# Softmax normalisation moved from the probabilities to the attention outputs, in a two-layer hybrid diffusion block on one core

## What is computed

```python
s = jnp.concatenate([s_win, s_ctx, sink_col], axis=-1)      # sink_col in the windowed heads only
p = jax.nn.softmax(s, axis=-1).astype(q.dtype)
o = einsum(p[..., :span], vw) + einsum(p[..., span:span + nctx], vc)
```

## Time and profile before

| | us |
|---|---|
| three runs | 1332.77, 1341.63, 1337.88 |
| median | 1337.88 |
| profiled execution, its own time | 1334.14 |
| its span, first to last instruction | 1332.3 |
| attention of layer 0, first scores to first gate product | 153.7 to 242.9 |
| attention of layer 1, the same | 874.7 to 931.0 |

### The profile page before, as it was taken

One profiled execution on the slowest core, in us unless ns is written; L12 is line 12 of the kernel. 1 busy time (PEld: TensorE's weight loads), 2 busy tenths in 40 slices (PEclk: granted clock), 3 DMA queues, 4 the chain that ended last, 5 costly groups with the idle time before them and its releaser, 6 DMA issues.

```text
span 1332.3 us, 22176 instructions
## 1 busy us (share of the span) xinstructions
PE 1213.0 (91%) x8966; PEld 927.0 (70%) x8966; DVE 645.4 (48%) x1503; ACT 440.1 (33%) x1049; POOL 167.0 (13%) x208
## 2 busy tenths in 40 slices
PE   4899987999999999999999889999998878889986
PEld 2787854788888967666666459875998865555652
DVE  1544786464355463422221285587767645324334
ACT  3533366533334351010000265356666610000001
POOL 1810000110010210000000321000111100000001
PEclk9899999999999999999999999999999889999998
DMA  9995145423323269999999995338564989999995
GB/s 352 316 353 177 64 138 188 150 95 95 95 95 127 90 265 416 399 415 413 416 384 373 402 237 149 120 133 278 177 189 145 357 333 413 417 416 413 380 374 192
DMA packets 131831, 351.15 MB, mean 264 GB/s; under 512 B 23053, under 2 KB 84725, under 8 KB 108560
## 3 DMA queue, kind: packets, MB, share of 16 engines
q1 hardware_dynamic: 118144, 317.69, 64.4%
q0 software_dynamic: 12304, 30.37, 6.7%
q10 hardware_dynamic: 1280, 1.66, 0.4%
HBM read 330.53 MB, written 28.86 MB: 270 GB/s over the span
## 4 chain that ended last, share of the span: by engine, by line
PE 81%; DVE 10%; issue 4%; DMA 4%; ACT 2%; POOL 0%; SPq 0%; DVEq 0%; ACTq 0%; POOLq 0%
PE banks L1028 34%; PE banks L1286 16%; PE banks L1300 8%; PE banks L1278 6%; PE banks L1209 4%; PE banks L962 2%; PE banks L1134 2%; PE banks L1149 2%; PE banks L1119 1%; DMA expert_rows<-arena,rows_u 1%; DMA ring<-in_w_in 1%; DMA ring<-in_w_mod 1%; DVE w_lo_r L2042 1%; DVE arena L2461 1%; DVE att L2128 1%
## 5 line engine op out<-in xcount | busy, mean ns | idle before, releaser
L2042 DVE TENSOR_TENSOR w_lo_r<-ring,w_hi_r 128x256 fp32r<-128x256 f32 x480 | 223.0, 475 | 229.5 <-ACT w_hi_r L1641 228.3
L1641 ACT ACTIVATE w_hi_r<-ring 128x256 fp32r<-128x256 f32 x480 | 197.5, 416 | 302.5 <-PE banks L1028 255.3
L1286 PE MATMUL banks<-ring,arena 128*64 128x256 f32 x2016 | 232.5, 383 | 21.5 <-DVE arena L2429 8.6
L1028 PE MATMUL banks<-h_hi_r,w_hi_r 128*128 128x512 f32 (+1 forms) x640 | 221.9, 347 | 5.7 <-DVE h_lo_r L1988 5.6
L1028 PE MATMUL banks<-h_lo_r,w_hi_r 128*128 128x512 f32 (+1 forms) x640 | 220.2, 344 | 0.0
L1028 PE MATMUL banks<-h_hi_r,w_lo_r 128*128 128x512 f32 (+1 forms) x640 | 220.0, 344 | 0.0
L1286 PEld LDWEIGHTS banks<-ring,arena 128*64 128x64 f32 x2016 | 161.9, 138 | 81.7 <-issue 31.2
L1028 PEld LDWEIGHTS banks<-h_hi_r,w_hi_r 128*128 128x128 f32 x640 | 122.3, 191 | 22.2 <-ACT arena L1611 5.0
L1300 PE MATMUL banks<-ring,att 128*64 128x512 f32 x424 | 119.7, 609 | 15.2 <-issue 7.8
L1028 PEld LDWEIGHTS banks<-h_lo_r,w_hi_r 128*128 128x128 f32 x640 | 122.5, 191 | 13.9
L1028 PEld LDWEIGHTS banks<-h_hi_r,w_lo_r 128*128 128x128 f32 x640 | 122.4, 191 | 13.9
(11 more groups left out here) (274 smaller groups left out, 1704.3 us busy)
## 6 DMA issues: line engine op xcount, KB each, us to landing
ring<-in_w_e_gate SPq DMA_DIRECT2D x64, 1024.0 KB, 8.9
ring<-in_w_e_up SPq DMA_DIRECT2D x62, 1024.0 KB, 9.3
ring<-in_w_e_down SPq DMA_DIRECT2D x53, 1024.0 KB, 9.3
ring<-in_w_mod SPq DMA_DIRECT2D x48, 1024.0 KB, 6.5
ring<-in_w_in SPq DMA_DIRECT2D x38, 1024.0 KB, 5.6
expert_rows<-att POOLq DMA_DIRECT2D x23, 512.0 KB, 20.3
ring<-in_w_o SPq DMA_DIRECT2D x8, 1024.0 KB, 5.1
ring<-in_w_branch SPq DMA_DIRECT2D x8, 640.0 KB, 4.6
```

The costliest lines, as they stand in the source:

```text
L1028: ins = mm(out_ap, a, b, start=k == 0 and p_ == 0, stop=k == KD - 1 and p_ == 2)
L1286: ins = mm(banks[e * CAP:(e + 1) * CAP, bank, 0:DE], x[:, k, e * CAP:(e + 1) * CAP], w[:, k * DE:(k + 1) * DE], start=k == 0, stop=k == KD ...
L1641: fn(w_hi[:, u % AHEAD, :, :], chunk(key)[:, q * KU:(q + 1) * KU, :], ACT.Copy).then_inc(w_hi_ready, 1)
L2042: v.tensor_tensor(w_lo[:, u % AHEAD, :, :], chunk(key)[:, q * KU:(q + 1) * KU, :], w_hi[:, u % AHEAD, :, :].bitcast(F32), ALU.subtract).th ...
```

## The change

The probabilities stay unscaled. VectorE still takes the reciprocals of the row sums, and then one copy spreads the two reciprocals of a step (two blocks of 128 queries) over 64 columns each, into `recip`, a view of arena tile 4 with room for two pairs of steps. At the end of `attend`, PE makes two products of `recip` with the identity: they turn it, so that bank 6, columns 256 to 511, holds for each output row of the two heads the reciprocals along the queries. ScalarE copies the raw outputs to `arena` as before (now counted by `o_raw`), and VectorE multiplies them by these columns once for two steps, behind the maximum of the even iterations (`o_ready`). `turn_p` waits for the exponentials instead of the scaling. The stream of VectorE is one iteration longer. In iteration 1 VectorE waits for `y_a_ready`. `small_in` and `gate_a_in` become one counter each over both layers. Matmul shapes, score and value products, and everything outside attention are as before.

```diff
+        recip = arena[:, T_AC, :].rearrange("p (u b e m) -> p u b e m", u=2, b=2, e=2)
@@ small parameters and gate rows
-        small_in = [sem(f"small_in{l}") for l in range(DEPTH)]
+        small_in = sem("small_in")
-        gate_a_in = [sem(f"gate_a_in{l}") for l in range(DEPTH)]
+        gate_a_in = sem("gate_a_in")
-                pool.wait_ge(small_in[l], SMALL)
+                pool.wait_ge(small_in, SMALL * (l + 1))
-                dve.wait_ge(gate_a_in[l], 16 * (2 - l))
+                dve.wait_ge(gate_a_in, 16 * (2 + l))
@@ PE, turn_p
-                pe.wait_ge(p_ready, g + 1)
+                pe.wait_ge(exp_done, g + 1)
@@ PE, attend
+                pe.wait_ge(recip_ready, g + 2)
+                for b in range(2):
+                    ins = mm(banks[:, O_BANK, (2 + b) * P:(3 + b) * P],
+                             recip[:, g // 2 % 2, b, :, :].rearrange("p e m -> p (e m)"), ident, start=True, stop=True)
                 ins.then_inc(pv_done, 1)
@@ ACT, attention
-                        fn(arena[:, tn, q0:q0 + 2 * P], banks[:, O_BANK, 0:2 * P], ACT.Copy).then_inc(o_ready, 1)
+                        fn(arena[:, tn, q0:q0 + 2 * P], banks[:, O_BANK, 0:2 * P], ACT.Copy).then_inc(o_raw, 1)
@@ DVE, attention
                     if 0 <= s - 1 < n:
-                        b = (s - 1) % 3
-                        k = width(l, s - 1) - (STEPS[l][s - 1][0] == "win")
+                        if s == 1:
+                            dve.wait_ge(y_a_ready, 2 * (l + 1))
                         dve.wait_ge(exp_done, g)
-                        link(v.reciprocal(rsum[:, b, :], esum[:, b, :]))
-                        for q in range(2):
-                            ins = v.tensor_scalar(S[b][:, q, 0:k], S[b][:, q, 0:k], rsum[:, b, q:q + 1], None, ALU.mult)
-                        ins.then_inc(p_ready, 1)
+                        r = rsum[:, (s - 1) % 3, :]
+                        link(v.reciprocal(r, esum[:, (s - 1) % 3, :]))
+                        v.tensor_copy(recip[:, (g - 1) // 2 % 2, :, (s - 1) % 2, :], r.unsqueeze(2).to_broadcast([P, 2, HD]))\
+                            .then_inc(recip_ready, 1)
...
                             .then_inc(max_ready, 1)
+                    if s % 2 == 0 and 0 <= s - 4 < n:
+                        family, h, on_ctx = STEPS[l][s - 4]
+                        tn = T_NQ + h // 2 if family == "na" else T_WQ + h % 3
+                        q0 = SEQ if on_ctx else 0
+                        o = arena[:, tn, q0:q0 + 2 * P]
+                        dve.wait_ge(o_raw, (g - 4) // 2 + 1)
+                        v.tensor_tensor(o, o, banks[:, O_BANK, 2 * P:4 * P], ALU.mult).then_inc(o_ready, 1)
@@ DVE, main
-                attention(l, 2, len(STEPS[l]) + 2)
+                attention(l, 2, len(STEPS[l]) + 3)
```

More of the change, by code:

```diff
@@ L473, in program @@
         exp_done = sem("exp_done")
-        p_ready = sem("p_ready")
+        recip_ready = sem("recip_ready")
         p_turned = sem("p_turned")
@@ L478, in program @@
         pv_done = sem("pv_done")
+        o_raw = sem("o_raw")
         o_ready = sem("o_ready")
@@ L625, in small_loads @@
             ):
-                eng.dma_start(dst, src).then_inc(small_in[l], 16)
+                eng.dma_start(dst, src).then_inc(small_in, 16)
         def load_rev(eng, l, heads=range(H_NA)):
@@ L934, in _ @@
                     pool.wait_ge(y_gated, QT0[1])
-                rows_in(l, 2, gate_bc, gate_a_in[l])
+                rows_in(l, 2, gate_bc, gate_a_in)
                 merge(l)
```

## The result

| | before | changed |
|---|---|---|
| median of 18 runs each (us) | 1335.61 | 1340.28 |
| lowest to highest | 1332.7 to 1342.2 | 1337.3 to 1344.66 |
| ratio, 95% interval | | 1.0033, 1.0019 to 1.0047 |
| profiled execution: own time, span | 1334.14, 1332.3 | 1344.66, 1342.8 |
| attention of layer 0 (first scores to first gate product) | 89.17 | 94.92 |

A forecast was written before the change was run, and what follows sets the result against it. The prediction took a loop of waits through `attend` to bound layer 0, with PE full in layer 1; 14 x 0.47 = 6.6 less 1.0 at the starts gave +5.6 us, forecast 1343.5, range 1334 to 1352.

The forecast's parts named there:

- The loop: Layer 0 latent pair: `attend`, turn, context scores, their copy, maximum, exponentials, copy of PT follow without idle, 8.05 us.
- Scaling, 0 in steady state, -0.52 at each start: Scaling gone from VectorE: hidden by 0.03 us in steady state; the second maximum starts 0.52 us earlier in each layer.
- Products, 0.47 a pair: Two identity products on PE at the end of `attend`, on the loop: between 0.39 and 0.66 us, taken as 0.47.
- Spreading copy, 0.20: VectorE's copy spreading the reciprocals, 0.20 us in a row, replacing 0.83 of scaling: 0 on the path.
- Output product, hidden with 0.2 of cover: VectorE's output product delays its copy of PT, but ScalarE's copy ends 0.2 us later: cost 0.
- Rival 3: Output product holds VectorE's queue, delaying PT's copy and `attend`; products may be dearer: +13.8 us, 1351.7, chance 0.11.
- The sum over the intervals: 10 `attend` intervals in layer 0 and 4 in layer 1, each +0.47: 6.6 us.
- The ends: Last stretch of each attention stage: the win at `turn_p` is taken back by the last products, about 0.
- Rivals 1, 2 and 4: 1: normalisation on path, 1334.7, chance 0.10; 2: VectorE bound, 1325.4, 0.08; 4: products under other PE work, 1336.9, 0.05.
- Rival 2: VectorE bounds the latent steps, so time goes with its work: -12.5 us, 1325.4, chance 0.08.

The follow-up runs named there:

- the second timing: The changed kernel, unaltered, timed again beside the two new orders against the kernel before: 1341.29 us, ratio 1.0037.
- the new order: Kernel before, PE's odd iterations with turn and context scores first, `attend` last, third PT buffer, ScalarE's output copy one iteration later: 1334.7 us, ratio 0.9996.
- the gap: Changed kernel with the two products moved from the end of `attend` to PE's idle time behind the modulation products in even iterations: 1335.15 us, ratio 0.9982.

## Why the prediction was right

The forecast was +5.6 us, 0.4% over the median of three runs; measured is +4.4 (2.5 to 6.3), and +4.9 by the ratio of the second timing (1.0037). The absolute time, 1340.28 for 1343.5, is off by 3.2 us, of which 2.3 are the base: the median of 18 runs of the kernel before is 1335.61 and not 1337.88. Step by step:

- **The loop is the bound of layer 0**: held. 8.54 for 8.05, the 0.10 ahead of `attend` and the 0.03 ahead of the maximum are in the trace of after. The two experiments that take one part each show it: products alone 8.54, scaling gone 8.11. And the new order, which takes `attend` off the loop and changes no work, brings the pair to 7.60.
- **Scaling, 0 in steady state, -0.52 at each start**: held. From the first scores to the first `attend` layer 0 took 14.21 us for 14.71, layer 1 14.10 for 14.62. One interval of layer 0, the seventh, went against it: there the scaling was on the path, and taking it away is worth 0.46 or more (5.75 and 5.73 for 6.21).
- **Products, 0.47 a pair**: 0.49. The four records stand 0.55 in a row, and the turn behind them is 0.05 shorter. Both lie inside the bounds 0.39 and 0.66 from rows, of which the lower one came from products of 96 columns and fewer (L1264), not 128. By the four passes of the Trainium skill ("FP8 and Floating Point Precision", TensorE Precision Notes) the estimate was 0.43, which was low.
- **Spreading copy, 0.20**: 0.23 as recorded, 0.2 or a little less in a row (181.16 and 0.23 in the rows above), hidden.
- **Output product, hidden with 0.2 of cover**: hidden, but the cover was looked for on one path only. Towards VectorE's copy of PT it is 0.24; by the bias and PE's latent scores it is 0.02, and the prediction didn't look at that path. Rival 3 fell all the same.
- **The sum over the intervals**: 14 intervals at 0.47 were to give 6.6. In layer 1 four intervals gave 1.98 (1.88 forecast), and the stage as a whole +1.57 (forecast +1.36). In layer 0 the first ten gave 6.06, or 4.4 without the clock (4.7 forecast): the seventh, with 6.22 for 6.21, paid nothing, since what the products cost there (6.53 with the scaling kept) the scaling gave back. The ends, forecast 0, cost 0.19 and 0.11. That the stages come within 0.1 us of the forecast's sum is in part luck: one interval less, against 0.02 more for each of the others and 0.3 at the ends.
- **Rivals 1, 2 and 4** are out by the run without the scaling (8.11, not 7.9 or less) and by that with the products alone. Rival 2, which the Trainium skill's "Perfetto Trace Analysis" (Identifying the Most-Contended Engine) spoke for, is out by the trace of after as well: VectorE's busy time fell from 21.5 to 17.8 of 24 us, and the pair grew. Even with `attend` off the loop, where VectorE is busy for 22.29 of 24 us, the step is set by a loop over VectorE and ScalarE (3.80 us).

What wasn't foreseen is the fall of the clock. It isn't part of a reason why the forecast held; without it the stages are 5.7 us longer, against 5.6. That PE's idle time ahead of the fifth `attend` would become one piece once the turn no longer waited for the scaling could have been seen; whether the clock then falls was open, and it falls in 4 of 9 such executions (last section).

Where expectations failed, it was for kernels with the new order: the latent pairs of layer 0 were worked out, and layer 1 was taken as unchanged. It was not (58.0, 60.5 and 58.8 us), since moving `attend` also moved what stands around it in the queues of the other engines, the emptying of bank 6 above all.

## What to carry to other kernels

Where no engine is full, follow one iteration back from its last wait until it closes, and price an edit only by what it puts on that loop; idle time with a releaser's name on it (0.77 us on the scaling here) is worth nothing unless it lies there. Work that must be added to an engine belongs in its idle time and not in front of the instruction that others wait for: the same two products cost a latent pair of layer 0 0.49 us behind `attend` and 0.02 in the gap. When an order is changed, look at each layer or stage by itself, and count the single-buffered places (here bank 6) whose emptying must move with it. And when added work is called hidden, follow every path that leaves it: here the one that was checked had 0.24 us to spare, the other 0.02.

## What the runs showed of the hardware

- **After PE had idled for 2 us the clock fell in some executions and not in others.** Of the executions with such a stretch in layer 0, it fell in both of the changed kernel (1.99 us idle, 1.6 us lost), in that without the scaling (2.05 idle) and in one of five with the new order in the kernel before (2.13), but not in that without products (1.99) nor in the other four of these (2.13 and 2.14): 4 of 9. Stretches of 4 us from the execution with the new order in which it fell:

```profile
214.00:218.00 4.00, 1.91 (x24) 0.83 (x20) 2.60 (x9) 2.12 (x8) 0.00 (x0) 1.00 0.61 205
218.00:222.00 4.00, 3.96 (x21) 1.99 (x22) 2.63 (x8) 2.52 (x9) 0.00 (x0) 0.67 0.70 239
```

And from its twin, the same kernel, after the same 2.13 us of idle:

```profile
214.00:218.00 4.00, 2.19 (x26) 0.98 (x22) 2.61 (x9) 2.41 (x8) 0.00 (x0) 1.00 0.61 205
218.00:222.00 4.00, 3.67 (x32) 2.30 (x36) 3.11 (x11) 2.35 (x8) 0.00 (x0) 1.00 0.75 257
```

  Why it falls in the one and not in the other stays open; how often it falls in the runs that were not profiled isn't known either.
- **A copy within SBUF of 128x128** with a broadcast source took 0.23 us on VectorE, where a product of two such operands took 0.29.
- **A hand-over of the same kind took 0.03 us or 0.09.** The maximum started 0.03 us after ScalarE's copy where VectorE had a scaling or a spreading copy ahead of it, and 0.09 after it in the run without either. The cause wasn't tried.
